# The three LayerNorms of a two-group encoder layer redone, and the gate columns put into the first weight pieces

## The chip, the cores and the metric

One core of one Trainium2 chip. The metric is the device time of one launch in microseconds (us); lower is better. The runs shown are of the same program on the same chip.

## The reference, cut to what matters

384 token rows (256 of a prompt, 128 of eight running streams of 16) of width 2048 go through one layer in fp32:

```
x   = layer_norm(x, ln_in_g, ln_in_b)
p   = x @ w_in                         # 3 x 1024 fox q,k,v | 8 forget gates | 3 x 1024 gdn q,k,v | 8 a | 8 b | 1024 z
o   = concat(8 forgetting-attention heads(p), 8 gated-DeltaNet heads(p)) @ w_out
x   = layer_norm(ALPHA * x + o, ln_mix_g, ln_mix_b)
h   = (silu(x @ w_gate) * (x @ w_up)) @ w_down        # 5632 hidden columns
y   = layer_norm(ALPHA * x + h, ln_ffn_g, ln_ffn_b)
```

`layer_norm(x, g, b) = (x - mean) * rsqrt(var + 1e-5) * g + b`, per row. Beside y the kernel returns keys, values, the logs of the forget gates, the DeltaNet states and the last rows of the convolution.

## The kernel before, in words

**Tiles and pieces.** The 384 rows are three tiles (TT = 3) of 128 in `x_res`. Every large product takes the activations transposed, `aT_hi` and `aT_lo` (16 slices of 128 channels by 384 rows), and the weights in pieces of 128 rows by 512 columns (384 for the forgetting heads). SyncE (SP) loads a piece into one of 8 slots of `raw` (`loads`, L185 to L191), ScalarE rounds it to a high half `w_hi` (`split_act`, L226), VectorE takes the low half `w_lo` (`split_dve`, L231), each into a ring of 4, and TensorE does three products for each tile (`gemm`, L244: hi x hi, hi x lo, lo x hi), so nine per piece. ScalarE and VectorE are three pieces ahead of TensorE.

**Blocks and courses.** The pieces make one long stream: 8 blocks of 16 pieces for the forgetting heads, 8 for the DeltaNet heads, 8 short blocks of 8 pieces for `w_out` (first half of its rows, then second), then the FFN in two halves (6 and 5 column blocks of gate and up, each half followed by 4 blocks of `w_down`). While the block of head h + 1 is multiplied, the attention or DeltaNet work of head h runs between its pieces. What is done where is written by hand: each engine has a `Course`, a generator whose `yield n` names a slot, and three slots (one for each tile) go by per piece. An engine's queue runs strictly in order, so a wait in a course also holds the splits that stand behind it.

**Opening.** SP loads the three tiles of x and the rows g and b of the first LayerNorm, broadcast to 128 partitions (L543 to L546); GpSimd (POOL) loads all constants, the gate columns `wg` and small things (L555 to L571). For each tile VectorE takes the moments (`row_stats` L285, `moments_dve` L291 to L296, with a three-step `rsqrt`, L265 to L270). Then a chain goes through 12 quarters (128 rows by 512 columns): ScalarE normalises (`normalise_act`, L307), VectorE multiplies by g (`scale_dve`, L315), POOL adds b (`shift_pool`, L322), TensorE transposes four 128 x 128 blocks (`x_transpose_pe`, L337), ScalarE and VectorE evacuate them as `aT_hi` and `aT_lo` (L348, L353). Only behind it stands the block of head 0. Between the pieces of that block stands the gate course (`gates_pe`, `gates_act`, `gates_dve`): 48 products with `wg` (L436), and, from slot 20 on, the transposes back, Exp, Ln and Tanh, and the decay sums as 30 small products (L453).

**Middle.** After the last `w_out` block (evacuated at L1399) the same chain of 12 quarters runs once more (`ln1_act`, `ln1_dve`, `ln1_pool`, `ln1_pe`), and the FFN's first piece stands behind all of it.

**End.** After the last `w_down` block (evacuated at L1567) the moments and the chain of ScalarE, VectorE and POOL run once more, without transposes (`end_act`, `end_dve`, `end_pool`), and SP stores each quarter (L1668).

## Time and profile before

| | |
|---|---|
| runs | 2086.29, 2087.13, 2090.3 us (median 2087.13) |
| the profiled execution's own time | 2089.48 us |
| its span | 2087.8 us, mean granted TensorE clock 0.982 |
| TensorE busy | 94% of the span |
| VectorE, ScalarE, GpSimd busy | 51%, 37%, 9% |
| DMA | 249.82 MB, mean 120 GB/s |

The span is what the profiler saw between the first and the last instruction; the execution's own time lies 1.7 us above it. PE is TensorE's matmul side, PEld its weight load, DVE VectorE, ACT ScalarE. The granted clock is a share of 2.4 GHz: 1.00 is that level, 0.50 is 1.2 GHz. A busy span of a product runs into that of the next, so the step from one start to the next is what a product costs.

### The profile page before, as it was taken

Reading aid. Unit: us, or ns where it says so; the run is one execution under the profiler, and the core shown is the slowest. Engines: PE = TensorE matmul, PEld = TensorE weight load, DVE = VectorE, ACT = ScalarE, POOL = GpSimd, SP = SyncE. Lnnn points to the kernel's source line nnn. Section 1 sums busy time; section 2 is a strip of 40 time slices with the busy share of each in tenths; the row PEclk is TensorE's granted clock in tenths of the full one; section 3 lists DMA queues with packets and bytes.
Section 4 is the critical chain, followed back from the end, with each engine's and each line's share of the span. In section 5 each row is a group of like instructions: output and inputs, shape, how many; then the busy total and the mean of one; then the engine's idle time right before and its main releaser. Section 6 shows DMA issues by size and latency. Waiting matters only on the chain.

```text
span 2087.8 us, 32037 instructions
## 1 busy us (share of the span) xinstructions
PE 1963.7 (94%) x9970; PEld 1634.1 (78%) x9970; DVE 1071.0 (51%) x2274; ACT 774.2 (37%) x1538; POOL 187.5 (9%) x263
## 2 busy tenths in 40 slices
...
GB/s 171 81 141 143 141 149 134 93 93 98 98 98 98 91 95 76 126 157 81 126 122 131 126 126 125 127 125 129 128 127 131 126 125 124 122 131 126 126 121 101
DMA packets 235946, 249.82 MB, mean 120 GB/s; under 512 B 21624, under 2 KB 154720, under 8 KB 234608
## 3 DMA queue, kind: packets, MB, share of 16 engines
...
q8 instruction: 32, 0.52, 0.1%
...
## 4 chain that ended last, share of the span: by engine, by line
PE 81%; DVE 10%; issue 4%; ACT 2%; DMA 1%; POOL 1%; DVEq 0%; POOLq 0%; ACTq 0%; SPq 0%
PE bank L244 71%; DVE work_a L1170 2%; DVE w_lo L231 2%; DMA x_res<-in_x_prompt 1%; ACT w_hi L226 1%; PE bank L1008 1%; POOL x_res L322 1%; PE bank L1502 1%; PE bank L1002 1%; PE bank L1028 1%; DVE x_res L315 1%; DVE pol L267 0%; DVE pol L268 0%; PE bank L436 0%; PE bank L1022 0%
## 5 line engine op out<-in xcount | busy, mean ns | idle before, releaser
L231 DVE TENSOR_TENSOR w_lo<-raw,w_hi 128x512 fp32r<-128x512 f32 x848 | 588.1, 700 | 750.8 <-ACT w_hi L226 747.0
L226 ACT ACTIVATE w_hi<-raw 128x512 fp32r<-128x512 f32 x848 | 526.8, 630 | 835.7 <-PE bank L244 835.5
L244 PE MATMUL bank<-w_hi,aT_hi 128*128 128x512 f32 (+1 forms) x1824 | 721.7, 396 | 8.5 <-DVE w_lo L231 5.8
L244 PE MATMUL bank<-w_hi,aT_lo 128*128 128x512 f32 (+1 forms) x1824 | 694.3, 381 | 0.0
L244 PE MATMUL bank<-w_lo,aT_hi 128*128 128x512 f32 (+1 forms) x1824 | 693.2, 380 | 0.0
L244 PEld LDWEIGHTS bank<-w_hi,aT_hi 128*128 128x128 f32 x1824 | 345.2, 189 | 74.9 <-DVE w_lo L231 16.3
L244 PEld LDWEIGHTS bank<-w_hi,aT_lo 128*128 128x128 f32 x1824 | 344.2, 189 | 57.5
L244 PEld LDWEIGHTS bank<-w_lo,aT_hi 128*128 128x128 f32 x1824 | 345.5, 189 | 47.5
L244 PE MATMUL bank<-w_hi,hT_hi 128*128 128x512 f32 x528 | 206.9, 392 | 0.6 <-DVE x_res L1567 0.5
L244 PE MATMUL bank<-w_hi,hT_lo 128*128 128x512 f32 x528 | 205.9, 390 | 0.0
L244 PE MATMUL bank<-w_lo,hT_hi 128*128 128x512 f32 x528 | 205.8, 390 | 0.0
L322 POOL TENSOR_TENSOR x_res<-x_res,raw 128x512 f32<-128x512 f32 x12 | 19.5, 1658 | 1104.7 <-DVE x_res L315 1104.7
L244 PEld LDWEIGHTS bank<-w_hi,hT_hi 128*128 128x128 f32 x528 | 99.2, 188 | 23.1 <-issue 1.7
L244 PEld LDWEIGHTS bank<-w_hi,hT_lo 128*128 128x128 f32 x528 | 99.2, 188 | 20.8
L244 PEld LDWEIGHTS bank<-w_lo,hT_hi 128*128 128x128 f32 x528 | 99.2, 188 | 20.2
L244 PE MATMUL bank<-w_hi,mixT_hi 128*128 128x512 f32 x192 | 78.8, 410 | 4.9 <-DVE x_res L1399 4.4
L337 PE MATMUL bank<-cn,x_res 128*128 128x128 f32 x96 | 26.5, 432 | 55.5 <-POOL x_res L322 34.5
L244 PE MATMUL bank<-w_lo,mixT_hi 128*128 128x512 f32 x192 | 75.7, 394 | 0.0
L244 PE MATMUL bank<-w_hi,mixT_lo 128*128 128x512 f32 x192 | 75.6, 394 | 0.0
L337 PEld LDWEIGHTS bank<-cn,x_res 128*128 128x128 f32 x96 | 17.2, 217 | 64.4 <-issue 43.4
L1170 DVE SCALAR_TENSOR_TENSOR work_a<-early,cw,work_a 128x384 f32<-128x384 f32 x72 | 44.6, 620 | 20.5 <-POOL early L1298 14.1
L1521 DVE TENSOR_TENSOR hT_lo<-bank,hT_hi 128x512 f32 (+1 forms) x33 | 22.8, 692 | 55.8 <-ACT hT_hi L1513 55.8
...
## 6 DMA issues: line engine op xcount, KB each, us to landing
...
raw<-in_w_in SPq DMA_DIRECT2D x128, 192.0 KB, 2.4
raw<-in_w_in SPq DMA_DIRECT2D x128, 128.0 KB, 2.2
raw<-in_w_in SPq DMA_DIRECT2D x256, 64.0 KB, 2.2
...
```

The lines of the kernel that those rows point to most:

```text
L226: nc.scalar.activation(w_hi[:, g % RING], raw[:, g % RAW], ACT.Copy).then_inc(sem("w_high"), 1)
L231: nc.vector.tensor_tensor(w_lo[:, g % RING], raw[:, g % RAW], w_hi[:, g % RING], ALU.subtract).then_inc(sem("w_split"), 1)
L244: last = nc.tensor.matmul(acc[t][:, 0:width], l[:, k0 + n, t * P:(t + 1) * P], r[:, g % RING, 0:width], start=(n == 0 and j == 0), stop=(n ...
L315: nc.vector.tensor_tensor(x, x, gb[0][:, c], ALU.mult).then_inc(sem("ln_scaled"), 1)
L322: nc.gpsimd.tensor_tensor(x, x, gb[1][:, c], ALU.add).then_inc(sem("ln_done"), 1)
L337: last = nc.tensor.transpose(bank[6 + r % 2][:, k * P:(k + 1) * P], x_res[:, t, c:c + P], ident)
L1002: nc.tensor.matmul(tl(b4, 0), A[:, 0, :], U[:, 0, :], start=True, stop=True)\
L1008: last = nc.tensor.matmul(tl(b6, t), A[:, t, :], U[:, t, :], start=True, stop=True)
L1028: last = nc.tensor.matmul(tl(b7, t + 1), T[:, t, :], Z[:, t, :], start=True, stop=True)
L1170: ins = V.scalar_tensor_tensor(out=out, in0=ext[:, a, :, r:r + NQ], scalar=w, in1=out, op0=ALU.mult, op1=ALU.add)
L1502: ins = nc.tensor.transpose(bank[6 + t % 2][:, k * P:(k + 1) * P], hb[:, t, k * P:(k + 1) * P], ident)
L1521: nc.vector.tensor_tensor(hT_lo[:, ks, cs], four(bank[6 + t % 2]), hT_hi[:, ks, cs], ALU.subtract).then_inc(sem("h_bank"), 1)
```

## The change

All three LayerNorms are done in another way, and the gates' product is no longer one of its own.

**First and middle LayerNorm.** ScalarE (tile 0) and VectorE (tiles 1 and 2) only bring x to mean 0 and variance 1 (`ln_unit_act`, `ln_unit_dve`), a quarter of the columns at a time. TensorE transposes one slice of 128 channels for all three tiles (`ln_turn_pe`); channels now lie on partitions, so ScalarE applies g and b as a column each while it evacuates (`ln_val_act`), and VectorE makes both halves (`ln_halves_dve`). The first two turns stand ahead of the next block's first piece, turn k + 2 stands between the tiles of piece k, and `gemm` waits for its own slice (`ready`). x_res itself gets g and b later: after the first LayerNorm by two VectorE instructions of 128 x 768 at slot 18 of each forgetting head, after the middle one by 24 POOL instructions of 128 x 512, one for every 6 pieces of the FFN's first half.

```diff
+        def ln_unit_act(q):
+            x = ln_quarter(q, 0)
+            nc.scalar.activation(x, x, ACT.Identity, scale=rstd[:, 0:1], bias=shift[:, 0:1])\
+                .then_inc(sem("n_unit_act"), 1)
+
+        def ln_unit_dve(q):
+            for t in (1, 2):
+                x = ln_quarter(q, t)
+                nc.vector.tensor_scalar(x, x, rstd[:, t:t + 1], shift[:, t:t + 1], ALU.mult, ALU.add)\
+                    .then_inc(sem("n_unit_dve"), 1)
+
+        def ln_turn_pe(pe, norm, k):
+            units = QUARTERS * norm + k // 4 + 1
+            pe.wait_ge(sem("n_unit_act"), units)
+            pe.wait_ge(sem("n_unit_dve"), 2 * units)
+            if k >= 2:
+                pe.wait_ge(sem("n_val"), KD * norm + k - 1)
+            for t in range(TT):
+                last = nc.tensor.transpose(bank[6 + k % 2][:, t * P:(t + 1) * P],
+                                           x_res[:, t, k * P:(k + 1) * P], ident)
+            last.then_inc(sem("n_ps"), 1)
+
+        def ln_val_act(act, norm, k, xt, gbc):
+            act.wait_ge(sem("n_ps"), KD * norm + k + 1)
+            if k >= 2:
+                act.wait_ge(sem("n_low"), KD * norm + k - 1)
+            nc.scalar.activation(xt[:, k % 2, :], bank[6 + k % 2][:, 0:TOK], ACT.Identity,
+                                 scale=gbc[:, 0, k:k + 1], bias=gbc[:, 1, k:k + 1]).then_inc(sem("n_val"), 1)
+
+        def ln_halves_dve(dve, norm, k, xt):
+            dve.wait_ge(sem("n_val"), KD * norm + k + 1)
+            nc.vector.tensor_copy(aT_hi[:, k, :], xt[:, k % 2, :]).then_inc(sem("n_high"), 1)
+            dve.wait_ge(sem("n_high"), KD * norm + k + 1)
+            nc.vector.tensor_tensor(aT_lo[:, k, :], xt[:, k % 2, :], aT_hi[:, k, :], ALU.subtract)\
+                .then_inc(sem("n_low"), 1)
 
...
+                    yield 18 + later
+                    dve.wait_ge(sem("gb_in"), 32)
+                    part = bass.ds(h * (D // HEADS), D // HEADS)
+                    for n, op in ((0, ALU.mult), (1, ALU.add)):
+                        after(nc.vector.tensor_tensor(
+                            x_res[:, :, part], x_res[:, :, part],
+                            gb0w[:, n, part].unsqueeze(1).broadcast_to([P, TT, D // HEADS]), op))
+                    yield 24 + later
...
+            def ln1_act(act):
+                for n in range(A_ACT):
+                    split_act(act, G_UP0, n)
+                act.wait_ge(sem("gb1_in"), 32)
+                act.wait_ge(sem("ln_moments"), 2)
+                ln_unit_act(0)
+                for k in range(KD):
+                    ln_val_act(act, 1, k, xt, gb1)
+                    if k % 4 == 1 and k // 4 + 1 < QUARTERS:
+                        ln_unit_act(k // 4 + 1)
+                    split_act(act, G_UP0 + A_ACT, k)
+
+            def ln1_dve(dve):
+                moments_dve(dve, range(TT))
+                dve.wait_ge(sem("ln_moments"), 2)
+                ln_unit_dve(0)
+                for k in range(KD):
+                    ln_halves_dve(dve, 1, k, xt)
+                    split_dve(dve, G_UP0 + 1, k)
+                    if k % 4 == 1 and k // 4 + 1 < QUARTERS:
+                        ln_unit_dve(k // 4 + 1)
+                for n in range(1, A_DVE):
+                    split_dve(dve, G_UP0 + NP_IN, n)
+
+            def ln1_pe(pe):
+                def turns():
+                    for k in range(2, KD):
+                        yield SLOTS * (k - 2) + 1
+                        ln_turn_pe(pe, 1, k)
+                for _ in range(WARM):
+                    nc.tensor.matmul(bank[5][:, :], ident, cn[:, 0:CW], start=True, stop=True)
+                ln_turn_pe(pe, 1, 0), ln_turn_pe(pe, 1, 1)
+                gemm(pe, G_UP0, NP_IN, aT_hi, aT_lo, 0, CW, ACC, "acc", BLK_MIX, between=Course(turns()),
```

**Opening.** The x loads (six halves) stand ahead of everything but two small ones; POOL loads only the unit matrix first and waits for the last half before the rest. `memset` covers only the unused columns of `raw`. The gate columns ride in the pieces of head 0, whose blocks are 408 columns wide (`GATES`), by two more DMAs per piece. The work on the gates (`gates_act`, `logs_dve`, `gates_pe`, `decays_act`, `sums_dve`) moves into head 1's block, where the course of head 0 is put 5 slots later. The g and b for x_res (two broadcasts of 1 MB) are loaded in SP's queue ahead of piece 18. Splits of the forgetting heads are 384 wide instead of 512. 20 small products on the unit matrix stand ahead of the first turn, 6 of 512 columns ahead of the middle one.

```diff
-            return [(r[:, 0:2, :], head_columns(n * P, FQ, 2, h)), (r[:, 2:3, :], head_columns(n * P, FV, 1, h))]
+            parts = [(r[:, 0:2, :], head_columns(n * P, FQ, 2, h)), (r[:, 2:3, :], head_columns(n * P, FV, 1, h))]
+            if isinstance(h, int) and h == 0:
+                for c, c0, c1 in ((3 * HD, FF, GQ), (3 * HD + 8, GA, GZ)):
+                    parts.append((raw[:, slot, c:c + c1 - c0], w_in[n * P:(n + 1) * P, c0:c1]))
+            return parts
...
+                    for n, v in enumerate((ln_in_g, ln_in_b)):
+                        sp.dma_start(lnrows[n * KD:(n + 1) * KD, :], v.rearrange("(k p) -> k p", p=P))\
+                            .then_inc(sem("rows_in"), 16)
+                    half = D // 2
+                    for t in range(TT):
+                        src = x_prompt[0, t * P:(t + 1) * P, :] if t < 2 else x_sample.rearrange("b s d -> (b s) d")
+                        for c in range(2):
+                            sp.dma_start(x_res[:, t, c * half:(c + 1) * half], src[:, c * half:(c + 1) * half])\
+                                .then_inc(sem(f"x_in{t}" if t < 2 else f"x_in2_{c}"), 16)
+                    for n in range(RAW):
+                        loads(sp, n, n, fox_parts(0, n, n), first=True)
+                    for n in range(RAW, NP_IN + RAW + A_DVE):
+                        h, m = divmod(n, NP_IN)
+                        if n == NP_IN + 2:
+                            load_gb(sp, (gb0w[:, 0, :], gb0w[:, 1, :]), ln_in_g, ln_in_b)
+                        loads(sp, n, n % RAW, fox_parts(h, m, n % RAW))
+
...
+                    nc.gpsimd.memset(gbias[:], 0.0).then_inc(sem("bias_zero"), 1)
+                    pool_wait(pool, sem("bias_zero"), 1)
+                    pool_wait(pool, sem("x_in2_1"), 16)
+                    pool.dma_start(cwraw[:], gdn_conv_w[0].rearrange("r (c p) -> (r c) p", p=P))\
+                        .then_inc(sem("conv_in"), 16)
+                    for half in range(2):
+                        pool.dma_start(stc[half * 24:half * 24 + 24, :],
+                                       state_conv[0].rearrange("b r c -> (b r) c")[:, half * 12 * P:(half + 1) * 12 * P])\
+                            .then_inc(sem("conv_in"), 16)
+                    pool.dma_start(cn[:, C_ONE:], const_in[:, C_ONE:]).then_inc(sem("masks"), 16)
...
+                def start_act(act):
+                    act.wait_ge(sem("gb0_ps"), 1)
+                    nc.scalar.activation(gb0[:].rearrange("p a k -> p (a k)"), bank[5][:, 0:2 * KD], ACT.Copy)\
+                        .then_inc(sem("gb0_in"), 1)
+                    act.wait_ge(sem("ln_moments"), 1)
+                    ln_unit_act(0)
+                    split_act(act, G_FOX, 0, width=GATES)
+                    act.wait_ge(sem("gb0_in"), 1)
+                    ahead = 1
+                    for k in range(KD):
+                        ln_val_act(act, 0, k, xt0, gb0)
+                        if k % 4 == 1 and k // 4 + 1 < QUARTERS:
+                            ln_unit_act(k // 4 + 1)
+                        while ahead <= k + (A_ACT - 1 if k else 1):
+                            split_act(act, G_FOX, ahead, width=GATES if ahead < NP_IN else 3 * HD)
+                            ahead += 1
+                    while ahead < NP_IN + A_ACT:
+                        split_act(act, G_FOX, ahead, width=3 * HD)
+                        ahead += 1
+
...
+                                dve.wait_ge(sem(f"x_in2_{q // 2}"), 16)
+                            elif q == 0:
+                                dve.wait_ge(sem(f"x_in{t}"), 32)
+                            last = row_stats(t, q)
+                    link(dve, last)
+                    moments_dve(dve, range(TT))
+                    dve.wait_ge(sem("ln_moments"), 1)
+                    ln_unit_dve(0)
+                    split_dve(dve, G_FOX, 0, width=GATES)
+                    for k in range(KD):
+                        ln_halves_dve(dve, 0, k, xt0)
+                        split_dve(dve, G_FOX, k + 1, width=GATES if k + 1 < NP_IN else 3 * HD)
+                        if k % 4 == 1 and k // 4 + 1 < QUARTERS:
+                            ln_unit_dve(k // 4 + 1)
...
+                    def turns():
+                        for k in range(2, KD):
+                            yield SLOTS * (k - 2) + 1
+                            ln_turn_pe(pe, 0, k)
+                            if k == KD - 5:
...
+                    for _ in range(WARM_IN):
+                        nc.tensor.matmul(bank[4][:, 0:P], ident, ident, start=True, stop=True)
+                    ln_turn_pe(pe, 0, 0), ln_turn_pe(pe, 0, 1)
+                    gemm(pe, G_FOX, NP_IN, aT_hi, aT_lo, 0, GATES, ACC, "acc", 0, first=True, between=Course(turns()),
+                         ready=lambda n: pe.wait_ge(sem("n_low"), n + 1))
...
-                    yield 10
+                    if first:
+                        yield 9
+                        gates_pe(pe)
+                        yield 12
...
+                def first_evac(act, t):
+                    wait_acc(act, "acc", 0, t, G_FOX + NP_IN)
+                    nc.scalar.activation(fbuf[:, t, :], bank[t][:, 0:3 * HD], ACT.Copy)
+                    nc.scalar.activation(gate[:, t, :], bank[t][:, 3 * HD:GATES], ACT.Copy).then_inc(sem("acc_free"), 1)
```

**Blocks ahead of the middle and the last LayerNorm.** The last `w_out` and the last `w_down` block go tile by tile through their last four pieces, so that tile 0 is whole first:

```diff
+                for t in range(TT):
+                    product(n, t)
+            for t in range(TT):
+                for n in range(pieces - RING, pieces):
+                    product(n, t)
+
...
+                        stats_of_block(dve, c, TT * (2 * HEADS + NCB + 1 + c))
+                    for n in range(NP_HALF - A_DVE):
+                        split_dve(dve, G_OUT_LAST + A_DVE, n)
+                    blk = 2 * HEADS + 2 * NCB - 1
+                    for t in range(TT):
+                        if t == TT - 1:
+                            split_dve(dve, G_UP0, 0)
+                        out_evac(dve, blk, NCB - 1, t, 1.0)
+                        dve.wait_ge(sem("acc_free"), TT * blk + t + 1)
+                        last = row_stats(t, NCB - 1)
+                    link(dve, last)
...
-                for c in range(NCB):
+                for c in range(NCB - 1):
                     gemm(pe, G_DN1 + NP_DN[1] * c, NP_DN[1], hT_hi, hT_lo, 0, CW, ACC, "acc", BLK_DN[1] + c,
                          between=Course(hidden_pe(pe, FB[0] + FB[1] - 1, True)) if c == 0 else None)
+                c = NCB - 1
+                gemm_tiles_last(pe, G_DN1 + NP_DN[1] * c, NP_DN[1], hT_hi, hT_lo, 0, ACC, "acc", BLK_DN[1] + c)
```

**End.** VectorE alone: as each tile is whole it is added and its moments taken; between the steps of the `rsqrt` (x - mean) * g is done for the quarters, and one instruction each is left behind it. The g and b (2 MB) are loaded in SP's queue ahead of the second block of `w_down`, into a buffer of their own.

```diff
+            def centre(t, q):
+                x, c = x_res[:, t, q * CW:(q + 1) * CW], slice(q * CW, (q + 1) * CW)
+                nc.vector.scalar_tensor_tensor(out=x, in0=x, scalar=moments[:, t, 0:1], in1=gb_last[:, 0, c],
+                                               op0=ALU.subtract, op1=ALU.mult).then_inc(sem("y_centred"), 1)
+
...
+                units = ((t, q) for t in range(TT) for q in range(QUARTERS))
+                dve.wait_ge(sem("gb_in"), 64)
+                for t in range(TT):
+                    down_evac(dve, 1, c, t, blk)
+                    dve.wait_ge(sem("acc_free"), TT * blk + t + 1)
+                    link(dve, row_stats(t, c))
+                    link(dve, nc.vector.bn_aggr(moments[:, t, :], stats[:, t].rearrange("p a b -> p (a b)")))
+                    if t == 0:
+                        for _ in range(QUARTERS):
+                            centre(*next(units))
+
...
+                    t, x, cs = quarter(r)
+                    dve.wait_ge(sem("y_centred"), r + 1)
+                    nc.vector.scalar_tensor_tensor(out=x, in0=x, scalar=rstd[:, t:t + 1], in1=gb_last[:, 1, cs],
+                                                   op0=ALU.mult, op1=ALU.add).then_inc(sem("y_whole"), 1)
```

**Beside these.** In each DeltaNet head TensorE's wait ahead of the last two products of the stream states is for `g_S2_ps`, the event of its own product just issued, instead of `g_S01_ps`. The g and b columns of the middle LayerNorm are loaded by POOL (two DMAs of 4-byte elements) at the start of the DeltaNet stage; SP's broadcast load of them in the middle is gone. `mixT` is two buffers (`mixF`, `mixG`).

```diff
                     W("g_v1")
                     nc.tensor.matmul(tl(b3, 1), qkdT[:, 1, :], vn[:, 1, :], start=True, stop=True)\
                         .then_inc(sem("g_o_ps"), 1)
                     nc.tensor.matmul(b4[:, 0:P], ke[:, 1, :], vn[:, 1, :], start=True, stop=True)\
                         .then_inc(sem("g_S2_ps"), 1)
-                    W("g_S01_ps")
+                    W("g_S2_ps")
                     streams(2), streams(3).then_inc(sem("g_Ss_ps"), 1)
                     yield 47
...
+                    for n, v in enumerate((ln_mix_g, ln_mix_b)):
+                        pool.dma_start(gb1[:, n, :], v[0].rearrange("(k p) -> p k", p=P),
+                                       allow_slow_non_contiguous=True).then_inc(sem("gb1_in"), 16)
                     with pool.Fori(0, HEADS) as i:
```

## Rows read from the trace of the kernel before

**Rows 1.** head of the page: busy us (share of the span) xinstructions

```profile
span 2087.8 us, 32037 instructions
...
PE 1963.7 (94%) x9970; PEld 1634.1 (78%) x9970; DVE 1071.0 (51%) x2274; ACT 774.2 (37%) x1538; POOL 187.5 (9%) x263
```

**Rows 2.** one stretch: us, engines' busy us (xcount), PEclk, DMA share, GB/s

```profile
956.80:1500.00 543.20, 543.13 (x2427) 449.25 (x2426) 217.65 (x324) 184.23 (x299) 0.00 (x0) 1.00 0.43 126
```

**Rows 3.** timeline, opening: start us, us, engine, line, tiles [idle before <-releaser]

```profile
5.98 2.47 DVE L285 BATCH_NORM_STATS2 stats<-x_res 128x6 f32<-128x512 f32 x4 [0.61 <-DMA x_res<-in_x_prompt]
...
22.38 2.47 DVE L285 BATCH_NORM_STATS2 stats<-x_res 128x6 f32<-128x512 f32 x4 [3.08 <-DMA x_res<-in_x_prompt]
...
52.96 0.67 PE L244 MATMUL bank<-w_hi,aT_hi 128*128 128x384 f32 x1
```

**Rows 4.** timeline of the middle LayerNorm, the same columns

```profile
927.77 0.39 PE L244 MATMUL bank<-w_hi,mixT_lo 128*128 128x512 f32 x1
...
931.36 0.51 DVE L291 BATCH_NORM_AGGREGATE moments<-stats 128x2 f32<-128x24 f32 x3
...
934.27 2.93 ACT L307 ACTIVATE x_res<-x_res,shift,rstd 128x512 f32<-128x512 f32 x4 [7.48 <-DVE shift L296]
...
956.47 0.78 PE L244 MATMUL bank<-w_hi,aT_hi 128*128 128x512 f32 x1
...
957.87 0.39 PE L244 MATMUL bank<-w_hi,aT_hi 128*128 128x512 f32 x1
```

**Rows 5.** timeline of the end

```profile
2052.54 0.39 PE L244 MATMUL bank<-w_hi,hT_lo 128*128 128x512 f32 x1
...
2060.30 19.48 POOL L322 TENSOR_TENSOR x_res<-x_res,raw 128x512 f32<-128x512 f32 x12 [1104.65 <-DVE x_res L315]
```

**Rows 6.** timeline of the gate chain, columns as in rows 3

```profile
78.39 1.28 ACT L479 ACT_TABLE_LOAD   x1
...
79.95 1.28 ACT L480 ACT_TABLE_LOAD   x1
...
82.76 0.45 PE L244 MATMUL bank<-w_hi,aT_hi 128*128 128x384 f32 x1 [2.06 <-DVE w_lo L231]
```

**Rows 7.** short stretches with their granted clock (PEclk), columns as in rows 2

```profile
4.00:8.00 4.00, 0.00 (x0) 0.00 (x0) 3.39 (x5) 0.00 (x0) 3.40 (x7) 1.00 1.00 406
84.00:88.00 4.00, 4.00 (x19) 3.90 (x17) 1.61 (x5) 0.00 (x0) 1.35 (x2) 0.50 0.63 148
...
96.00:100.00 4.00, 4.00 (x20) 4.00 (x19) 1.23 (x4) 1.26 (x2) 0.00 (x0) 0.79 0.39 97
```

**Rows 8.** chain of waits around head 0: start us, us, what

```profile
86.14 6.34 PE bank L453 x30
...
105.38 0.33 PE bank L670 x3
105.71 1.06 PE bank L244 x6
```

**Rows 9.** groups, forms apart: line, engine, tiles, shapes, count | busy us, mean ns

```profile
L231 DVE TENSOR_TENSOR w_lo<-raw,w_hi 128x512 fp32r<-128x512 f32 x848 | 588.1, 700 | 750.8 <-ACT w_hi L226 747.0 <-DVE hb L1548 2.0
...
L307 ACT ACTIVATE x_res<-x_res,shift,rstd 128x512 f32<-128x512 f32 x36 | 27.3, 803 | 41.4 <-DVE shift L296 41.4
...
L1211 DVE TENSOR_TENSOR early<-early,cn 128x384 f32<-128x384 f32 x8 | 4.5, 558 | 0.3
...
L436 PE MATMUL bank<-aT_hi,wg_hi 128*24 128x384 f32 x16 | 5.8, 361 | 0.0
...
L819 DVE TENSOR_SCALAR fo<-fo,frs 128x128 f32<-128x128 f32 x24 | 5.4, 283 | 0.3
...
L1062 PE MATMUL bank<-work_a,ke 128*128 128x128 f32 x16 | 3.1, 275 | 0.0
```

**Rows 10.** head 0's block, columns as in rows 2

```profile
103.80:135.70 31.90, 31.21 (x216) 30.00 (x215) 18.69 (x55) 14.52 (x32) 4.36 (x6) 1.00 0.52 136
```

**Rows 11.** DMA issues: tile, queue, count, KB each, us to landing

```profile
work_a<-in_ln_mix_g SPq DMA_DIRECT2D x1, 1024.0 KB, 4.6
```

649 lines of the change are left out of this document (307 added, 342 removed).

## The prediction

> **What bounds the kernel now.** I read the head of the page first: TensorE is busy for 1963.7 of 2087.8 us [rows 1], far ahead of every other engine. Then the busy time of long stretches: in the first FFN half TensorE is busy for 543.13 of 543.20 us at a granted clock of 1.00 [rows 2], so nothing can be won there by another engine, and time has to come from where TensorE waits. The timeline shows three such places. In the opening the first product starts at 52.96 [rows 3]. In the middle the last product starts at 927.77 and, a step of about 0.23 on (543.13 us for 2427 products, a few of them short ones [rows 2]), is done by 928.0; the next block starts at 956.47 [rows 4]: 28.5 us. At the end the last product is done by 2052.8 [rows 5] and the span ends at 2087.8: 35.0 us. Together 116 us, and the change works on all three. A fourth place is the gate chain in head 0's block: two table loads of 1.28 us on ScalarE hold its splits, TensorE idles 2.06 us, and soon after its granted clock falls to 0.50, 1.2 GHz, for some 13.5 us (0.50 at 84 to 88; the mean of 0.79 at 96 to 100 has it back at 97.7) [rows 6, 7]. At half speed 13.5 us cost 6.75. The 30 decay sums took 6.34 us there [rows 8], half of it clock.
>
> The sum is made against the profiled execution, 2089.48 us (span 2087.8 and 1.7 around it); that is 2.35 above the median of the three runs, and I take that off at the end. The runs lie within 0.2% of each other, so less than that can't be told from no change.
>
> **Opening, step by step.** (a) Tile 0 of x, issued at 1 us, was there at 5.98, but tile 1 only at 22.38 [rows 3], since 2 MB of broadcasts and POOL's constants went ahead of it. Now x is alone. DMA moved 406 GB/s in this stretch [rows 7], so 3 MB need some 8 us behind a start near 4: all of x at 12. VectorE's statistics, 12 at 0.62 (four took 2.47), start at about 6.9 and are done at 14.4; the rest of the moments took 2.9 in the middle (931.36 to 934.27) [rows 3, 4]: 17.3. Then a quarter to unit variance (ScalarE 0.80 [rows 9], VectorE's two bounded by 0.57 and 1.40, that is two of the 128-wide form or two of the 512-wide two-input form), a turn of three transposes at 0.23 (half speed), the evacuation 0.6 (384 columns, under the 0.80 of 512), the two halves 1.0 with their events: first product at 21.3, where it was at 52.96. Minus 31.6. Bounds: 18 and 27, the latter if the first weight pieces crowd x. (b) 48 gate products go; 384 columns at full clock step 0.175 (six in 1.06 [rows 8]): minus 8.4. The 24 columns that every product of the block gets instead cost 144 x 0.175 x 24/384 = 1.6. (c) 14 turns stand inside the block. Three transposes took 0.33 at full clock [rows 8]; with the change of operand I take 0.38, so 5.3 (0.69 each at half speed would make 9.7). Before, they stood ahead of the block, where they cost nothing of their own. (d) Beside them per piece: VectorE copies and subtracts 384 columns, splits 408 and now and then units, at most 0.56 + 0.56 + 0.60 + 0.3 = 2.0 by [rows 9], against TensorE's nine products and a turn, 1.68 + 0.38 = 2.06. Close, but TensorE still ends last. By the Trainium skill (VectorE: DVE Perf Modes, "The perf-mode tier table") fp32 copies and tensor-scalars out of SBUF run at twice the rate and two-input ones do not; the 0.283 of L819 is too short a form to show it. The sum would be about 1 us lower by it. Opening: -31.6 - 8.4 + 1.6 + 5.3 = -33.1.
>
> **Gates, moved.** Table loads, decay sums and the clock's fall go from head 0's to head 1's block. ScalarE there does two more evacuations, then Exp, Ln and Tanh with the same two loads (2.56 us), then its first query copy, all ahead of the split of the fourth piece, which TensorE wants 5.4 us in and gets at about 7.5: again 2.1 us of idling, again a fall of 6.75, and the key rows wait some 1 us for the column that follows the sums. Taken: +1. Bounds: -7 (no fall) to +5.
>
> **Forgetting heads.** The new x work is two instructions of 768 columns on VectorE per head; from 700 for 512 and 558 for 384 [rows 9] one takes 0.98, so 2.0 per head. Its 16 splits of 128 columns less give back 16 x 0.14 = 2.3. VectorE was busy for under 60% of head 0's 31.9 us [rows 10]. Zero; what hides it is the lead of three pieces, 4.7 us.
>
> **Middle.** With tile 0 and 1 whole 5.4 and 2.7 us ahead of the end (24 and 12 steps), VectorE has one tile left: add 0.7, statistics 0.7, the chain 2.9, unit up to 1.3, turn 0.5, evacuation 0.6, halves 1.0, events 0.4: 8.1, call it 8.2 for 28.5. Minus 20.3. Turns inside: 14 x 0.38 = +5.3. Clock: before it was back at full speed at 957.87, 1.4 us into the block, so 0.7 were lost. Now 6 products of 512 keep TensorE going for 2.6 us and it then idles for about 3. After 2.06 us of idling it fell, so I expect a fall, of between 2 us and the 13.5 of [rows 7]: +3 (bounds -0.7 and +6.8). VectorE per piece: 1.1 for halves, 0.7 split, under TensorE's 2.04 + 0.38. The POOL work on x_res, 24 instructions, goes beside the FFN, where it doubles VectorE's splits while it runs; that half has VectorE idle for over half its time [rows 2]. Zero. Middle: -12.0.
>
> **End.** Counted from the last product: tile 1's work ends at +0.65, tile 2's evacuation, statistics and aggregation at 2.3; eleven small steps at 0.2 with eight quarters at 0.62 between them: 9.5; twelve last instructions: 17. Before, the last POOL instruction ended at 2079.8 [rows 5], 8.0 ahead of the span's end, for store and close; and since stores of 256 KB now come each 0.62 us, near the rate of the DMA, I add 1. 26 for 35.0: minus 9 (bounds -6 and -10.5). The 2 MB in SP's queue ahead of the weights need 5 us at 406 GB/s; a broadcast of 1 MB landed 4.6 us after its issue in the middle [rows 11]. The loads are 5 pieces (10 us) ahead of the splits' lead. Just covered: zero, at worst 3.
>
> **DeltaNet heads.** TensorE now waits for the end of its own product: a product of this size steps by 0.11 and ends after 0.275 [rows 8, 9], so 0.17 with the event make about 0.25, times 8: +2 (bounds 0 and 4).
>
> **Sum.** -33.1 + 1 - 12.0 - 9 + 2 = -51.1. 2089.5 - 51.1 = 2038.4, and against the median 2036.
>
> **Rivals.** (A) The forecast, 2036. (B) The opening block is fed late. For: its pieces have 256 more short runs each (32 and 64 bytes), and masks, caches and the 2 MB for x_res, 4.1 MB, come at the same time. Head 0's block kept all DMA engines busy for 0.52 of 31.9 us for 136 GB/s, 4.3 MB [rows 10], so a piece of 384 runs of 512 bytes (0.197 MB) took 0.76 us of them; 256 more at the same or twice the price of a run make 1.3 to 1.8 per piece, 16 of them 20 to 28, and 10 us for the 4.1 MB: 30 to 38, as long as the block itself (37). Against: the loads have a lead of 8 pieces. If they are late: 5 us and one more fall of 6.8: 2048. By the Trainium skill (DMA: Bandwidth & Descriptors, "Specifications") line rate wants 512 bytes or more and below it there is a read-modify-write, which speaks for (B) by the dearer of the two prices. (C) The clock stays up in head 1's block or in the middle: -6.8 and -3, 2026. For: the sums and warming products fill the pauses; against: the fall after 2.06 us. By the Trainium skill (TensorE: Matmul & The Clock Gate, "What's actually happening") the slow level is the default and activity lifts it. The trace agrees in the step lengths, not in the granted column, which says 1.00 before TensorE had done anything. (D) Slower than before: the x work at slot 18 makes VectorE late in every head. It decides from the point where TensorE idles there by the 2.06 us of [rows 6]: then each of 8 heads pays 2.1 and a fall of 6.8, 71 in all, 2107. Against: 13 us of idle VectorE in head 0's block, and TensorE idle for only 0.7 of its 31.9 us [rows 10]. (E) The change doesn't do what it says: turns and products don't overlap, and each piece waits for its turn, evacuation and halves, 2.1 us, 28 times: 2095. Against: turn k + 2 is issued in piece k.
>
> **How the numbers follow.** A 0.52, B 0.23, C 0.20, D 0.02, E 0.02, and 0.01 for no change. Faster by over 0.2%: 0.95. Slower: 0.04. The range takes in C with 4 us for the lower bounds of opening and end, 2022, and B with 6 for the upper ones, 2054.
>
> **What would show it.** First product near 21, head 0's block some 37 us long with TensorE busy throughout; L453 and both table loads in head 1's block with a granted clock of 0.50 behind them; a gap of 8 us between the last mixG product and the first of the FFN; 26 us behind the last product. Wrong if TensorE's waits for w_lo in the opening add up to over 5 us, if first products start after 27, or if any forgetting head is longer than 33 us.

## The result, and the profile after

Four runs of the changed kernel took 2018.34 to 2021.01 us, median 2019.89; beside them four of the kernel before took 2086.29 to 2090.3, median 2087.53. The ratio is 0.9674, 95% interval 0.9657 to 0.969: 67.6 us less. The forecast was 2036 with a range of 2022 to 2054, so the sign was right and the gain was 16 us larger than worked out, just outside the range. The profiled execution took 2021.01 us, with a span of 2019.4.

From the head of the page of the changed kernel, its answer to [rows 1]:

```profile
span 2019.4 us, 32098 instructions
PE 1951.9 (97%) x9972; PEld 1625.6 (80%) x9972; DVE 1065.0 (53%) x2308; ACT 747.3 (37%) x1520; POOL 165.3 (8%) x260
```

The timeline of TensorE in the opening and in the middle (start, duration), the answer to [rows 3, 4]:

```profile
11.74 7.24 PE L540 MATMUL bank<-cn 128*128 128x128 f32 x40 [6.37 <-DMA x_res<-in_x_sample]
19.14 0.85 PE L356 MATMUL bank<-cn,x_res 128*128 128x128 f32 x6 [0.17 <-DVE x_res L346]
21.57 0.42 PE L255 MATMUL bank<-w_hi,aT_hi 128*128 128x408 f32 x1 [1.58 <-DVE aT_lo L371]
21.83 0.35 PE L255 MATMUL bank<-w_lo,aT_hi 128*128 128x408 f32 x1
...
885.77 0.39 PE L275 MATMUL bank<-w_hi,mixG_lo 128*128 128x512 f32 x1
886.00 5.31 PE L1592 MATMUL bank<-cn 128*128 128x512 f32 x12
891.71 0.85 PE L356 MATMUL bank<-cn,x_res 128*128 128x128 f32 x6 [0.40 <-DVE x_res L346]
894.02 0.57 PE L255 MATMUL bank<-w_hi,aT_hi 128*128 128x512 f32 x1 [1.47 <-issue]
```

First product at 21.57, and already at full speed: the next ones step by 0.19 for 408 columns. The middle's gap runs from 886.0 to 894.02. An fp32 product of 512 columns is two records and takes 0.88, so the six warming products keep TensorE going for 5.31 us, where I had 2.6.

Head 1's block, in stretches of 4 us (busy us and number per engine, granted clock, DMA share, GB/s), the answer to [rows 7]:

```profile
54.00:58.00 4.00, 3.25 (x20) 3.04 (x20) 1.84 (x7) 3.14 (x10) 0.00 (x0) 1.00 0.90 241
58.00:62.00 4.00, 3.76 (x26) 3.45 (x25) 2.13 (x10) 3.96 (x10) 2.40 (x4) 1.00 0.26 52
62.00:66.00 4.00, 4.00 (x32) 4.00 (x31) 1.07 (x3) 0.72 (x2) 2.34 (x4) 0.85 0.87 238
66.00:70.00 4.00, 4.00 (x17) 3.90 (x16) 1.91 (x10) 1.33 (x5) 0.00 (x0) 0.50 0.43 143
70.00:74.00 4.00, 4.00 (x21) 3.95 (x20) 2.14 (x6) 0.52 (x1) 0.00 (x0) 0.80 0.41 98
```

TensorE's pauses are 0.75 and 0.24 us, where it had idled for 2.06 [rows 6]. The clock still falls, but the half-speed shares (0.30, 1.00 and 0.40 of the last three stretches) add up to 6.8 us instead of 13.5.

And the end, the answer to [rows 5]; the last two are VectorE's last instructions and the issues of the stores:

```profile
1998.93 0.39 PE L275 MATMUL bank<-w_hi,hT_lo 128*128 128x512 f32 x1
2008.34 8.04 DVE L1833 SCALAR_TENSOR_TENSOR x_res<-x_res,rstd,gb_last 128x512 f32<-128x512 f32 x12
2009.12 7.62 SPq L1799 DMA_DIRECT2D out<-x_res  x12
```

From these rows and one event that both kernels have in every head (the first turn of the queries, L670 before and L695 after; the one in head 2's block started at 137.45 and at 96.20), the whole span divides as follows.

| stretch | before | after | measured | forecast |
|---|---|---|---|---|
| start to first product | 52.96 | 21.57 | -31.4 | -31.6 |
| blocks of heads 0 and 1 | 84.5 | 74.6 | -9.9 | -0.5 |
| to the last mixG product | 790.3 | 789.6 | -0.8 | +2 |
| gap in the middle | 28.5 | 8.0 | -20.5 | -20.3 |
| FFN | 1096.1 | 1104.9 | +8.8 | +8.3 |
| behind the last product | 35.0 | 20.2 | -14.8 | -9 |
| sum | | | -68.4 | -51.1 |

"Forecast" in the second row is the sum of -8.4, +1.6, +5.3 and +1. The third stretch ends at the start of the last mixG product, the gap begins at its end, 0.23 later. Two rows hold 15.2 of the 17.3 us of error: 9.4 in the blocks of heads 0 and 1, 5.8 at the end; 2.8 more are in the third. The runs look at these two, and at the steps that came out right, to see whether for the right reason.

### The profile page after: what moved, and what is told of

Same layout as the page of the kernel before. It is cut to its first block, busy times and chain, and to the rows that moved or that the text cites. A ratio compares the mean times of both kernels' runs of the same rounds, so it can differ in the third digit from the quotient of the medians.

```text
span 2019.4 us, 32098 instructions
## 1 busy us (share of the span) xinstructions
PE 1951.9 (97%) x9972; PEld 1625.6 (80%) x9972; DVE 1065.0 (53%) x2308; ACT 747.3 (37%) x1520; POOL 165.3 (8%) x260
## 4 chain that ended last, share of the span: by engine, by line
PE 82%; DVE 10%; issue 3%; ACT 3%; SPq 1%; DMA 1%; DVEq 1%; POOL 0%; ACTq 0%; POOLq 0%
PE bank L255 70%; PE bank L275 3%; DVE work_a L1248 2%; DVE w_lo L240 1%; ACT w_hi L235 1%; PE bank L1086 1%; SPq L196 1%; PE bank L1626 1%; PE bank L1080 1%; PE bank L1106 1%; PE bank L1100 0%; DVE pol L300 0%; DVE pol L299 0%; DVE x_res L1804 0%; DVE stats L317 0%
## 5 line engine op out<-in xcount | busy, mean ns | idle before, releaser
L240 DVE TENSOR_TENSOR w_lo<-raw,w_hi 128x512 fp32r<-128x512 f32 (+2 forms) x848 | 583.2, 694 | 684.2 <-ACT w_hi L235 680.1
L235 ACT ACTIVATE w_hi<-raw 128x512 fp32r<-128x512 f32 (+2 forms) x848 | 515.8, 616 | 833.7 <-PE bank L255 795.2
L255 PE MATMUL bank<-w_hi,aT_hi 128*128 128x512 f32 (+2 forms) x1824 | 723.4, 397 | 10.2 <-DVE w_lo L240 3.7
L255 PE MATMUL bank<-w_hi,aT_lo 128*128 128x512 f32 (+2 forms) x1824 | 693.3, 380 | 0.0
L255 PE MATMUL bank<-w_lo,aT_hi 128*128 128x512 f32 (+2 forms) x1824 | 692.5, 380 | 0.0
L255 PE MATMUL bank<-w_hi,hT_hi 128*128 128x512 f32 x468 | 183.1, 391 | 0.4 <-DVE x_res L1691 0.3
L255 PE MATMUL bank<-w_hi,mixF_hi 128*128 128x512 f32 x96 | 40.9, 426 | 4.9 <-DVE x_res L1480 4.4
L255 PE MATMUL bank<-w_hi,mixF_lo 128*128 128x512 f32 x96 | 38.3, 399 | 0.0
L255 PE MATMUL bank<-w_lo,mixF_hi 128*128 128x512 f32 x96 | 38.1, 397 | 0.0
L1386 POOL DMA_DIRECT2D out<-gbuf x64 | 35.6, 556 | 9.4 <-issue 8.5
```

Source lines behind the costliest of these rows:

```text
L235: nc.scalar.activation(w_hi[:, g % RING, 0:width], raw[:, g % RAW, 0:width], ACT.Copy).then_inc(sem("w_high"), 1)
L240: nc.vector.tensor_tensor(w_lo[:, g % RING, 0:width], raw[:, g % RAW, 0:width], w_hi[:, g % RING, 0:width], ALU.subtract).then_inc(sem("w_ ...
L255: last = nc.tensor.matmul(acc[t][:, 0:width], l[:, k0 + n, t * P:(t + 1) * P], r[:, g % RING, 0:width], start=(n == 0 and j == 0), stop=(n ...
L1386: pool.dma_start(o_cs[0, b].rearrange("r (a g c) -> r a g c", a=3, c=HD)[:, :, bass.ds(h, 1), :] .rearrange("r a o c -> r a (o c)"), gbuf[ ...
```

## The experiments

Each kernel is the changed one with the edit shown, unless said otherwise. Together with a second measurement (r_again) the changed kernel has nine runs, 2018.34 to 2021.01, median 2018.96; differences below are of medians against that. Some clock losses are a matter of chance, so a microsecond is at the limit of what these medians tell.

**1. No warming products in the opening.**

```
-WARM_IN = 20
+WARM_IN = 0
```

> Theory (the 20 small products on the unit matrix ahead of the first turn take the cold start away; the prediction had missed that and kept the slow start): without them the first products of head 0's block step by some 0.34 instead of 0.19 us for 408 columns, for some 4 to 7 us, head 0's block is 2 to 4 us longer than 33.4, and the whole run 2 to 4 us above the changed kernel (2022 to 2024). Rival (they do nothing, the clock would be up by itself because the turns come first): the steps stay at 0.19 and the time within 1 us of 2020.

Measured: 2019.76 us median of 5 (ratio 0.9678, 0.9664 to 0.9691), 0.8 more. Its timeline:

```profile
22.06 0.68 PE L255 MATMUL bank<-w_hi,aT_hi 128*128 128x408 f32 x1 [1.27 <-DVE aT_lo L371]
22.54 0.54 PE L255 MATMUL bank<-w_lo,aT_hi 128*128 128x408 f32 x1
22.88 0.54 PE L255 MATMUL bank<-w_hi,aT_lo 128*128 128x408 f32 x1
23.22 0.54 PE L255 MATMUL bank<-w_hi,aT_hi 128*128 128x408 f32 x1
```

The products step by 0.34 until 27.0, and from the first product to the first query turn it takes 36.35 us instead of 35.0. Those 35.0 hold the pause of 0.75 us at the start of head 1's block, which this execution does not have; the second profile of the changed kernel (experiment 8) doesn't have it either and takes 34.0. Like against like, the 20 products are worth 2.3 us, inside the theory's 2 to 4. In this execution the later losses of clock were smaller than in the profiled one of the changed kernel (3.4 us of half speed in head 1's block, none in the middle), so the median's 0.8 can't be taken as the price.

**2. No warming products in the middle.**

```
-WARM = 6
+WARM = 0
```

> Theory (the 12 records of products between the last mixG product and the turns keep most of the clock; the fall behind them cost 3.6 us at half speed): without them the pause of TensorE is 5.7 us and the slow stretch behind it is as long as those of the trace, 3.6 to 13.5 us, so the run is 0 to 5 us longer (2020 to 2025). Rival (they are useless, since the clock falls anyway at the start of the block): no difference, the slow stretch again ends at about 897.6.

Measured: 2021.2 us (0.9685, 0.9672 to 0.9698), 2.2 more. TensorE idles for 5.55 us ahead of the turns:

```profile
890.14 1.51 PE L356 MATMUL bank<-cn,x_res 128*128 128x128 f32 x6 [5.55 <-DVE x_res L346]
892.82 0.76 PE L255 MATMUL bank<-w_hi,aT_hi 128*128 128x512 f32 x1 [1.16 <-issue]
```

The granted clock is down for 10.2 us, of which 6.0 lie behind the first FFN product, against 3.4 us in the changed kernel's profile. The warming products are worth about 2 us.

**3. GpSimd ends last.**

```
                 ln1_pool(pool)
+                pool_wait(pool, sem("y_whole"), ROUNDS)
+                nc.gpsimd.memset(shift[:, 0:1], 0.0)
```

> One wait for the last of VectorE's last instructions and a small memset are put at the end of GpSimd's programme. Theory (in the kernel before, the 6.4 us between the landing of the last store and the end of the span belong to GpSimd, which ends last there and long before the end in the changed kernel): the span goes on for some 6 us behind the landing of the last store instead of 0.9, and the run is 3 to 6 us longer (2023 to 2026). Rival (the 6.4 us were SyncE's or the profile's): the run stays within 1 us of 2020 and the last store lands 0.9 us ahead of the end.

Measured: 2022.83 us, 2020.18 to 2026.18 (0.969, 0.9676 to 0.9703), 3.9 more at the median, and 2026.18 in the profiled execution, whose span ends at 2024.6. In its end the memset stands at 2017.06, the last store is issued by 2017.3, and all data have moved by 2018.5:

```profile
2014.28 2.98 SPq L1799 DMA_DIRECT2D out<-x_res  x5
2017.06 0.10 POOL L1854 MEMSET shift<- 128x1 f32 x1 [783.52 <-DVE x_res L1833]
DMA  9999999999999996200000000000000000000000
```

(The last line is the DMA's share in 40 equal slices of 0.265 us, from 2014 on.) 6.1 us follow in which nothing is seen, where the changed kernel has 0.9. The kernel before had them too; its last store's data have moved by 2081.4 and the span ends at 2087.8:

```profile
2080.00:2084.00 4.00, 0.00 (x0) 0.00 (x0) 0.00 (x0) 0.00 (x0) 0.00 (x0) 0.50 0.19 74
2084.00:2087.80 3.80, 0.00 (x0) 0.00 (x0) 0.00 (x0) 0.00 (x0) 0.00 (x0) 0.50 0.00 0
```

So a programme of GpSimd that works to the end costs some 3 to 6 us behind the last store (the profiled execution is the longest of the five). Why, no row shows; that one run of the five shows almost nothing of it (2020.18) stays open too.

**4. The last blocks in plain order.**

```
-                    gemm_tiles_last(pe, G_OUT_LAST, NP_HALF, ...)
+                    gemm(pe, G_OUT_LAST, NP_HALF, ...)
...
-                gemm_tiles_last(pe, G_DN1 + NP_DN[1] * c, ...)
+                gemm(pe, G_DN1 + NP_DN[1] * c, ...)
```

> The last w_out and the last w_down block go piece by piece instead of tile by tile at their end. In the prediction's sum all but the last tile's work lies ahead of the last product. Theory: in the middle the evacuation (0.7) and statistics (0.7) of two more tiles stand behind the last product, 2.8 us, part of which the 5.3 us of warming products cover only if VectorE is not the one that ends last (it is, so they cover nothing); at the end the same 2.8 us, plus four quarters that were centred ahead of the last product, 4 x 0.66. Sum 5 to 8 us, 2025 to 2028. Rival (the tile order is worth little, since the moments' chain and the last twelve instructions set the end): under 3 us, below 2023.

Measured: 2025.34 us (0.9706, 0.9693 to 0.9719), 6.4 more, within 5 to 8. The gap in the middle is 10.1 instead of 8.0, the end 24.4 instead of 20.2. Both places are 2 us dearer for two more tiles behind the last product, and the end 2 more for the centring that no longer fits ahead of it.

**5. The decay sums spread over three slots.** Theory N in the following is that the clock's fall in head 1's block goes with the 30 narrow sums; theory I, that it goes with the pauses.

```
                     sums(S_C + 16, [(LS, lf[:, 2, :])])
+                    yield 10
...
+                    yield 11
...
-                        yield 12
+                        yield 13
```

> The 30 decay sums (24 of them of 8 columns) are put into three slots with three weight products between each two groups, the key rows one slot later. Theory N (the clock's fall in head 1's block follows the narrow sums, in which TensorE works but moves few columns): the granted clock stays at 1.00 or falls for under 2 us, heads 0 and 1 take some 2 to 3 us less than the 74.6 us of the changed kernel, time 2017 to 2018.5. Theory I (it follows the two short pauses, 0.75 us at the head's start and 0.24 us ahead of the sums, as it followed the 2.06 us in the kernel before): the fall is there again for 3 to 7 us and the time within 1 us of 2020.

Measured: 2019.11 us (0.9673, 0.966 to 0.9687), 0.2 more. The stretch of half speed is 6.8 us long, as before:

```profile
62.00:66.00 4.00, 4.00 (x32) 4.00 (x31) 0.66 (x2) 0.31 (x1) 1.93 (x3) 0.90 0.90 232
66.00:70.00 4.00, 3.92 (x15) 3.41 (x16) 1.91 (x10) 1.22 (x5) 0.00 (x0) 0.50 0.37 127
```

Read alone this spoke for I.

**6. Wide products between the sums.**

```
                     def sums(col, pairs):
+                        nc.tensor.matmul(sums_ps[:, 288:512], ident, cn[:, 0:224], start=True, stop=True)
```

> A product of 224 columns on the unit matrix ahead of each of the 14 groups of sums, some 0.4 us each at the full clock, 5.5 us in all. Theory N: no fall, so minus 2.9 for it and plus 5.5 for the products, 2022 to 2023. Theory I: the fall stays where it is, 3 to 7 us long, and in it the products cost more: 2025 to 2027.

Measured: 2023.78 us (0.9689, 0.9676 to 0.9702), 4.8 more; and in head 1's block there is no fall:

```profile
62.00:66.00 4.00, 4.00 (x27) 4.00 (x27) 1.21 (x3) 0.85 (x2) 2.48 (x4) 1.00 0.91 232
66.00:70.00 4.00, 4.00 (x28) 4.00 (x28) 0.00 (x0) 0.00 (x0) 0.00 (x0) 1.00 0.49 149
```

The pauses ahead of them (0.24 us before the sums and the one at the block's start) were not touched. It is the only one of the profiles with a full clock here, and what N expects. The time by itself does not decide: 2023.78 lies between the ranges of N and I. The edit costs more than it gives. The stretch with the sums takes 8.2 us instead of 3.9, of which the products are 4.9 (3.3 is what the sums take at full clock), and a pause of 0.50 comes in behind it.

**7. One more product behind the middle's turns.**

```
                 ln_turn_pe(pe, 1, 0), ln_turn_pe(pe, 1, 1)
+                nc.tensor.matmul(bank[5][:, :], ident, cn[:, 0:CW], start=True, stop=True)
```

> One more product of 512 columns on the unit matrix behind the first two turns of the middle. It fills 0.9 of the 1.47 us in which TensorE waits ahead of the FFN's first product. Theory I: the fall behind the middle goes, 1.8 us less, 2018. Rival (the pause ahead of the turns, with the rows of zeros in the warming products, is enough for a fall): the slow stretch of 3 to 6 us is there again, 2020 to 2021.

Measured: 2019.28 us (0.9669, 0.9656 to 0.9682), no difference. There was no fall in the middle, but see the next run. And the time hides a loss elsewhere: in this execution the clock falls for 3.4 us right behind the first product of the opening, and from there to the first query turn it takes 35.6 us.

```profile
22.00:26.00 4.00, 3.91 (x14) 3.76 (x15) 3.11 (x8) 2.29 (x5) 0.00 (x0) 0.57 0.73 162
```

The pause of 1.58 us ahead of the first product is in the changed kernel as in this one. Of the fourteen profiles with the 20 products, two show this fall, this one and that of experiment 11.

**8. The changed kernel again.**

> The changed kernel once more, as the measure for differences of a microsecond: 2020 within 1.5. If the length of the slow stretch in head 1's block is a matter of chance, it is another than 7 us here, and heads 0 and 1 take 72 to 75 us.

Measured: 2018.96 us, 2018.75 to 2019.81 (0.9668, 0.9655 to 0.9681). Here the clock stays up in the middle with no edit at all:

```profile
892.00:896.00 4.00, 2.73 (x14) 2.28 (x15) 3.72 (x8) 1.96 (x4) 1.19 (x2) 1.00 0.46 146
896.00:900.00 4.00, 3.99 (x20) 2.98 (x19) 2.02 (x5) 2.38 (x4) 0.00 (x0) 1.00 0.41 122
```

The FFN took 1103.3 instead of 1104.9. Of ten profiles with this same pause, three show the fall there, each 3.4 us long; so experiment 7 settles nothing. Heads 0 and 1 took 73.8, again with 6.8 us of half speed; the 0.8 less are the pause at the start of head 1's block, which is not there.

**9. The splits of the forgetting heads 512 wide again** (`3 * HD` to `CW` in the four calls of heads 1 to 7).

> The splits of the forgetting heads 1 to 7 are 512 wide again instead of 384. In the trace of the kernel before TensorE waited 3.7 us for low halves in head 1 to 7's blocks, in the changed one 1.4, and those blocks are 2.1 us shorter in sum. Theory (the narrower splits pay for the two new instructions on x and give the 2 us besides): the stretch from head 0's first query turn in head 2's block to the last mixG product is 2 to 4 us longer than 789.4, with waits for w_lo of some 4 to 6 us; time 2021 to 2023. Rival (the 2.1 us are from the order of the courses): the stretch within 0.5 us of 789.4.

Measured: 2021.1 us of 4 (0.968, 0.9665 to 0.9695), 2.1 more. TensorE's waits for low halves from 97 to 888 us, in this kernel and in the changed one (in all, times, longest):

```profile
PE bank L255 <- DVE w_lo L240: 4.6, 14, 0.5
```

```profile
PE bank L256 <- DVE w_lo L241: 2.9, 14, 0.2
```

From the first query turn in head 2's block to the last one of the last forgetting head it takes 193.0 us here, 191.4 in the changed kernel, 193.0 in the kernel before. So 1.6 us are the narrower splits, as the theory had it. The longer stretch that the expectation named, up to the last mixG product, was only 0.1 to 0.2 longer, since this execution lacked another short fall of the clock, near 785 us, that all others but experiment 11's have.

**10. The 2 MB of g and b four pieces later.**

```
-                        if n == NP_IN + 2:
+                        if n == NP_IN + 6:
```

> The 2 MB of g and b for x_res go ahead of piece 22 in SyncE's queue instead of ahead of piece 18. Theory (the late DMA of rival B is what makes ScalarE wait 1.3 us for a piece, the evacuation late by 1.1 us and TensorE pause at the start of head 1's block, and this pause is part of what brings the clock down): the wait for the evacuation goes, minus 1.1 us, and where the fall goes too minus 2.5 to 3.5 more: heads 0 and 1 in 69.5 to 73 us, time 2015.5 to 2018. Rival (the pieces are then late in the middle of head 1's block instead): waits for w_lo behind 60 us, no gain, 2018.5 to 2020.

Measured: 2018.68 us (0.9666, 0.9653 to 0.9679), 0.3 less, too little to be told from nothing. In the profile of the changed kernel ScalarE's longest wait for a piece in 40 to 60 us, and TensorE's wait behind it at the start of head 1's block, are

```profile
ACT w_hi L235 <- DMA raw<-in_w_in: 2.3, 1, 2.3
PE bank L255 <- DVE w_lo L240: 0.7, 1, 0.7
```

and both are gone here, so the late DMA of rival B is real, and it did cost TensorE time. How much varies: of the twelve profiles without this edit, experiments 13 and 14 included, four have no such wait of ScalarE, two have 1.3 and 1.6 us of it and no pause of TensorE, five have 2.3 to 2.5 and a pause of 0.7 to 1.0, and one (experiment 13) has

```profile
ACT w_hi L235 <- DMA raw<-in_w_in: 3.6, 1, 3.6
PE bank L255 <- DVE w_lo L240: 2.1, 1, 2.1
```

In the three profiles with the edit (here, 11 and 15) neither is there. The wait for the evacuation that the theory names is another one, and it stays, the same in the changed kernel and here. It stands at 93.4 us, at the start of head 2's block:

```profile
PE bank L255 <- ACT fbuf L898: 1.1, 1, 1.1
```

So the theory is right on the late piece, about 1 us where it is 2.3 us late, and wrong on the evacuation and on the fall: half speed lasts 6.8 us without the pause too.

**11. Experiments 7 and 10 together, and two products of 224 columns ahead of the sums.**

> The same, with one more product of 512 columns behind the first two turns of the middle and two of 224 columns ahead of the decay sums, which stand where TensorE waits for the sums' data (0.24 to 0.29 us) and cost some 0.6 us beside it. Theory: no slow stretch in head 1's block nor in the middle: 2015 to 2017, and the runs closer together than those of the changed kernel, which spread by 2.7 us. Rival (the fall is set by more than these pauses, as the spread sums have it): a slow stretch of 3 to 7 us is still there, 2018 to 2020.

Measured: 2019.22 us, 2016.72 to 2021.49 (0.967, 0.9657 to 0.9683), no difference, and still 3.4 us of half speed, beside the 3.4 in the opening named under 7. The two products did not fill the pause: it is 0.31 us here, three weight products ahead of them. Wide products ahead of the sums do not keep the clock.

**12. The kernel before again.**

> The kernel before once more, for a second profile of it. If the length of the fall is a matter of chance: the slow stretch behind the gates in head 0's block is not 13.5 us, but between 4 and 14, and the run's time is lower than 2089.5 by half of what the stretch is shorter. Rival (13.5 belongs to the kernel): 13 to 14 us again. In both cases the last store lands some 6 us ahead of the span's end.

Measured: 2086.68 us, one run, span 2085.0. The fall in its head 0's block, where [rows 7] have 13.5 us:

```profile
82.00:86.00 4.00, 4.00 (x20) 3.91 (x18) 1.63 (x6) 0.00 (x0) 1.35 (x2) 0.54 0.59 143
86.00:90.00 4.00, 4.00 (x21) 4.00 (x20) 0.00 (x0) 0.00 (x0) 1.79 (x2) 0.50 0.54 150
90.00:94.00 4.00, 4.00 (x18) 4.00 (x18) 2.41 (x10) 1.55 (x5) 0.00 (x0) 0.68 0.55 183
```

0.92 + 1 + 0.64 of 4 us are 10.2 us. Heads 0 and 1 take 83.2 instead of 84.5, 1.3 less, where the shorter fall makes 1.7. So 13.5 was one draw, and I had built a term on it. The last data move 6.5 us ahead of the span's end, as in the first profile (6.4), and the pause of 2.06 us ahead of the fall is there again.

**13. The decay sums twice.** (The second time over the first.)

> The decay sums are made twice, the second time over the first: 60 small products instead of 30. Theory N (the fall follows the narrow sums): it starts while they run, some 2 to 3 us behind the first one as in the changed kernel, and the slow stretch is longer by the time that the second 30 take, 3 to 6 us, so heads 0 and 1 take 5 to 8 us more than 74: time 2024 to 2027. Theory I (it follows the pauses): the same stretch of 3 to 7 us, and 3.3 us for the products: 2022 to 2024.

Measured: 2025.11 us of 4 (0.9699, 0.9685 to 0.9714), 6.2 more, theory N's 5 to 8. In the profiled execution, the longest of the four, half speed lasts 10.2 us (1.84 + 4 + 4 and 0.4 in the stretch behind these), longer than in any profile of the changed layout with 30 sums:

```profile
66.00:70.00 4.00, 4.00 (x30) 4.00 (x29) 0.18 (x1) 0.00 (x0) 0.23 (x1) 0.77 0.82 233
70.00:74.00 4.00, 4.00 (x21) 4.00 (x20) 0.00 (x0) 0.00 (x0) 0.00 (x0) 0.50 0.04 12
74.00:78.00 4.00, 4.00 (x15) 3.90 (x15) 1.91 (x10) 1.33 (x5) 0.00 (x0) 0.50 0.00 0
```

It also has a fall of 3.4 us at 57 to 61, behind a pause of 2.1 us at the block's start, where TensorE waited for the low half of the piece that the DMA brought late (the lines under 10). So both kinds exist in this block; the one behind the sums grows with them.

**14. The sums merged.** lf, gl, glb and lc stand in one buffer `dk`; LP times 48 columns at once, ones times 128, and so on, 10 products instead of 15:

```
-                    sums(S_C, [(LP, lf[:, 0, :])])
...
+                    sums(S_C, [(LP, dk[:, 0:48])])
+                    sums(S_C + 8, [(LP, dk[:, 8:16]), (ones, dk[:, 0:8])])
...
+                    sums(S_TS, [(ones, dk[:, 48:176])])
```

> The logs of the gates stand in one buffer, and the decay sums are 10 products of 8 to 128 columns instead of 15 of 8 to 64 (20 instead of 30 in the profile). They take 1 us less. Theory N: the slow stretch is gone or shorter than 3 us, 2016 to 2017.5. Theory I: 3 to 7 us of it, 2017.5 to 2019.

Measured: 2016.3 us, 2015.38 to 2017.49 (0.9658, 0.9645 to 0.9671), 2.7 less than the changed kernel, and all five runs below its nine. Heads 0 and 1 take 71.0. The sums take 2.34 us:

```profile
61.72 2.34 PE L611 MATMUL bank<-dk,cn 128*128 128x48 f32 x20
```

and half speed lasts 3.4 us (0.21 + 0.21 of 4 us, counted twice):

```profile
62.00:66.00 4.00, 4.00 (x27) 4.00 (x27) 1.89 (x10) 1.12 (x6) 1.79 (x3) 0.79 0.84 209
66.00:70.00 4.00, 4.00 (x22) 3.85 (x21) 1.97 (x6) 0.92 (x2) 0.00 (x0) 0.79 0.57 189
```

A length of 3.4 us was also seen with 30 sums, in six profiles of eleven (6.8 in the rest), so this one doesn't show that the merge shortens the fall. The medians only point to it: the products alone are worth 1.1 us (2.15 from the first sum to the next weight product instead of 3.27 at full clock), and 2.7 was measured. The time is in N's range, but N's "gone" did not come true.

**15. Merged sums with experiments 7 and 10.**

> The merged sums, the g and b for x_res ahead of piece 22, and one more product of 512 columns behind the first turns of the middle. No slow stretch in the middle, and where theory N holds none in head 1's block: 2015 to 2017. Rival: the clock falls in head 1's block all the same, 2017 to 2018.5.

Measured: 2016.0 us, 2013.88 to 2017.89 (0.9654, 0.9641 to 0.9668). Not to be told apart from 14. The clock stays up in the middle, falls for 3.4 us in head 1's block, so the rival's condition holds, and for 6.8 near 785 us. These two are the fastest kernels of the study.

## Why the prediction was right and where it failed

**Opening.** Right, -31.4 for -31.6, and step by step: x there for the products at about 12, first turn at 19.14, first product at 21.57 (21.3).

**Blocks of heads 0 and 1: the failed step.** The prediction said of the gates, "again 2.1 us of idling, again a fall of 6.75", and it silently kept the slow start of head 0's block in its 37 us. Neither held. (1) The kernel before started at half speed: its first products step by 0.32 and 0.33 for 384 columns, until about 59.9, 6.9 us with 0.45 of idling in them, so some 3.3 lost. In the profile of the changed kernel none is lost; experiment 1 brings 2.3 back. The 20 products were in the diff and in my description, with no term for them. (2) The fall was taken as 13.5 us, from one execution, and as the same again in its new place. It is 6.8 here, so 3.4 us less is lost; experiment 12 shows that the length is not fixed even in one kernel (13.7 and 10.2 before), and the changed kernel and its variants have 3.4 or 6.8. (3) The 2.06 us of idling did not come back, only 0.24. With the other pauses in these blocks, 0.75 for the late piece and 1.09 for the evacuation against 0.45 and 0.69 before, TensorE idles for 2.1 us instead of 3.2. Both table loads hold ScalarE as I had it, but in head 1's block TensorE meanwhile turns head 0's queries, keys and cache, 14 transposes that head 0's block did not have; that they fill the pause is argued from the timeline, not tried. 3.3, 3.4 and, for idling, 1.1 make 7.8 of the 9.4. The 1 us for key rows that I had added did not show, and a turn of the LayerNorm costs 0.33 instead of 0.38 (one starts at 24.75, the products behind it at 25.00, 25.27 and 25.45, where they else step by 0.19), 0.6 for the 14. That is all of it.

**What makes the fall.** The profiles show falls behind pauses and falls behind narrow sums. In the kernel before it came 1.3 us behind a pause of 2.06, ahead of the sums. In the changed kernel it comes 2 to 4 us behind the start of the sums with no pause over 0.46 us right ahead of them; with wide products between them it goes (6, one profile), with twice as many it is 10.2 us (13), with two fillers ahead of them it stays (11). Experiment 5 doesn't fit the simple form of N: six weight products among 30 sums were not enough.

Its length follows an order that the clock records of the profiles show. It goes with how long the sums still take, at half speed, when the clock falls. In the eight profiles with 1.2 us or less to come it is 3.4 us long, in the five with 1.4 to 2.1 us 6.8, in the two with 6.4 (experiment 13) and 7.7 (12) 10.2, and in the first profile of before, with 8.2, it is 13.7. On this reading the fall before the change was long because the pause put its start ahead of all the sums, while afterwards most sums are done when it starts. No run was made to test it, and what sets the moment of the fall, 2.1 to 4.1 us behind the first sum in the changed layout, stays open.

By the Trainium skill (TensorE: Matmul & The Clock Gate, "What's actually happening") the slow level is the default and activity releases it. The traces agree for the start: in the kernel before the products step by 0.32 and then, from 60.15 on and with no pause between, by 0.17. They add that the clock can fall while the profile calls TensorE busy for 4.00 of 4.00 us, as in the row of 62 to 66 us of the changed kernel, where it makes the narrow sums.

**Forgetting heads.** Called zero, with the course hidden; measured 1.6 us less over six blocks. The mechanism that I named (splits narrower by 128 columns) was right, and I took it only as payment for the x work. Over these blocks the waits for low halves were 3.0 us before and 1.4 after, too small to be looked for, and they were the gain; with the wide splits of experiment 9 they are 3.0 again. D, the way to slower, was never near.

**DeltaNet heads.** +2 was forecast for the wait on its own product; over seven heads the trace has 399.0 us instead of 398.5. That most of the wait lay in the 0.275 that the product takes anyway is argued; no run had the other wait.

**Middle.** Gap 8.0 for 8.2. In the FFN +8.8 for +8.3, and that it came so near is luck: 1.7 us were lost by the fall against 0.7 before, so the clock's term was +1.0, or -0.7 where there is no fall as in experiment 8, and I had +3. The rest, 7.8 us, are the 14 turns with a few small waits, 0.56 each for my 0.38. In experiment 8's profile a turn starts at 897.14 and the products behind it at 897.38, 897.70, 897.93 and 898.34, where they else step by 0.23. That I took the warming products as half as long as they are did not show, since VectorE ended last either way. Experiment 2 makes them worth 2 us.

**End.** -14.8 for -9. VectorE's work went as forecast: counted from the last product's end, 1999.16, its twelve last instructions begin at 9.2 and end at 17.2; I had 9.5 and 17. Behind them stood 9 us, 8.0 taken over from the kernel before "for store and close" and 1 for stores near the rate of the DMA. It was 3.0, of which the stores take all but the last 0.9. Some 5.5 us of the 8.0 belonged to GpSimd as the last engine (experiment 3, and the same 6.4 in both profiles of before), and the change takes GpSimd out of the end. This is the second failed term: a stretch in which the profile shows nothing was carried over as if it belonged to the end of any kernel.

**Rivals.** B's late DMA is there in eight of twelve profiles, at the start of head 1's block. It costs TensorE nothing or 0.7 to 1.0 us, and once 2.1 us and a fall of 3.4 behind them (10, 13); B had 5 us and one more fall. C, the clock, was the nearest in number, with 2026, and had 0.20. Its condition held only in part: in head 1's block the clock fell in every profile but the one with wide products between the sums, only for less long, and in the middle it stayed up in seven of ten. The cold start and the closing, which make the rest, stood in no rival.
